# One core, two transformer blocks: the spatial stage written out by halves of the tokens, with some low parts subtracted by GpSimd

## The reference

```
proj = x @ w_in_2 + b_in_2            # u, v (part A, 512 each), a, b (part B, 512 each)
u, v = gelu(u), gelu(v)
v = layer_norm(v per head of 128, ln_a_g, ln_a_b)
v = tril(w_spatial[head]) @ v (per chunk of 128 tokens) + b_spatial[head]
part_a = u * v                         # "gated rows"
y = a * sigmoid(b)
y = causal_depthwise_conv(y, 31 taps, conv_b_w) + conv_b_b
part_b = silu(layer_norm(y over 512 channels, ln_b_g, ln_b_b))   # "conv rows"
out = concat(part_a, part_b) @ w_out_2 + b_out_2
x = layer_norm(alpha * x + out, ln1_g, ln1_b)
```

## Time and profile before

| | us |
|---|---|
| Median of 3 runs | 4498.53 |
| Lowest, highest | 4498.35, 4501.0 |
| Profiled execution | 4507.0 |
| Its span | 4505.3 |
| Busy PE, PEld, DVE | 3978.4, 3237.4, 2283.2 |
| Busy POOL, ACT | 1930.4, 1161.4 |

### The profile page before, as it was taken

How to read it: one execution, slowest core, us unless ns; L and a number is a source line. 1 busy time by engine, 2 the same in 40 slices (tenths; PEclk the granted TensorE clock), 3 DMA queues, 4 the chain that set the end, 5 groups by cost and what they waited for, 6 DMA issues and landing times.

```text
span 4505.3 us, 51892 instructions
## 1 busy us (share of the span) xinstructions
PE 3978.4 (88%) x18898; PEld 3237.4 (72%) x18898; DVE 2283.2 (51%) x3082; ACT 1161.4 (26%) x1863; POOL 1930.4 (43%) x754
## 2 busy tenths in 40 slices
PE   4778979999999899999997999999977467999997
PEld 3557767787887777777775778787866246888886
DVE  4763364344344655544545421222688876545556
ACT  3222122111114444443432211111321123222221
POOL 2323338455652412222212755564456244544551
PEclk9888979999999999999976999999988778999998
DMA  4320002223220110110100111111010010111111
GB/s 176 104 67 29 29 28 63 87 84 102 86 68 22 41 33 24 33 34 29 33 19 29 44 50 42 51 51 42 26 40 28 9 46 20 56 42 42 56 47 47
DMA packets 235628, 220.82 MB, mean 49 GB/s; under 512 B 11189, under 2 KB 188499, under 8 KB 234468
## 3 DMA queue, kind: packets, MB, share of 16 engines
q1 hardware_dynamic: 212401, 167.21, 12.3%
q10 hardware_dynamic: 23090, 51.74, 3.4%
HBM read 214.66 MB, written 4.26 MB: 49 GB/s over the span
## 4 chain that ended last, share of the span: by engine, by line
PE 74%; DVE 16%; issue 4%; ACT 3%; DMA 1%; POOL 0%; ACTq 0%; SPq 0%; DVEq 0%; POOLq 0%
PE PS L613 9%; PE PS L615 9%; PE PS L614 9%; PE PS L753 5%; PE PS L755 5%; PE PS L754 5%; PE PS L640 4%; DVE CX L2429 4%; PE PS L641 4%; PE PS L642 4%; PE PS L1066 3%; DVE QSQ L2241 2%; DVE ADMS L1862 1%; PE PS L1036 1%; PE PS L998 1%
## 5 line engine op out<-in xcount | busy, mean ns | idle before, releaser
L2671 POOL TENSOR_SCALAR WH<-RAW 128x1024 fp32r<-128x1024 f32 (+1 forms) x247 | 730.1, 2956 | 1427.2 <-PE PS L642 614.8
L613 PE MATMUL PS<-UH,WH 128*128 128x512 f32 (+1 forms) x2192 | 877.7, 400 | 25.4 <-POOL WL L2673 12.1
L615 PE MATMUL PS<-UH,WL 128*128 128x512 f32 (+1 forms) x2192 | 868.5, 396 | 0.0
L614 PE MATMUL PS<-UL,WH 128*128 128x512 f32 (+1 forms) x2192 | 862.7, 394 | 0.0
L1873 DVE TENSOR_TENSOR X<-PS,X 128x512 f32<-128x512 f32 x656 | 444.2, 688 | 493.7 <-PE PS L755 411.0
L2673 POOL TENSOR_TENSOR WL<-RAW,WH 128x1024 fp32r<-128x1024 f32 (+1 forms) x247 | 615.8, 2493 | 20.6
L613 PEld LDWEIGHTS PS<-UH,WH 128*128 128x128 f32 (+1 forms) x2192 | 417.5, 190 | 117.4 <-issue 15.7
L615 PEld LDWEIGHTS PS<-UH,WL 128*128 128x128 f32 (+1 forms) x2192 | 415.7, 190 | 98.4
L614 PEld LDWEIGHTS PS<-UL,WH 128*128 128x128 f32 (+1 forms) x2192 | 416.9, 190 | 93.4
L753 PE MATMUL PS<-WH,HH 128*128 128x512 f32 x1024 | 405.7, 396 | 33.6 <-DVE HL L2158 18.0
L755 PE MATMUL PS<-WL,HH 128*128 128x512 f32 x1024 | 400.3, 391 | 0.0
(11 more groups left out here) (343 smaller groups left out, 7307.3 us busy)
## 6 DMA issues: line engine op xcount, KB each, us to landing
RAW<-in_mlp_w_dram SPq DMA_DIRECT2D x128, 512.0 KB, 3.9
ADM<-in_ada_w_dram ACTq DMA_DIRECT2D x96, 256.0 KB, 3.1
RAW<-in_w_up_dram SPq DMA_DIRECT2D x44, 512.0 KB, 3.9
ADR<-in_ada_w_dram ACTq DMA_DIRECT2D x12, 1024.0 KB, 5.1
RAW<-in_w_down_dram SPq DMA_DIRECT2D x22, 512.0 KB, 3.3
RAW<-in_ev_w_in_dram SPq DMA_DIRECT2D x20, 512.0 KB, 4.0
ADS<-in_ada_w_dram SPq DMA_DIRECT2D x8, 1024.0 KB, 16.1
WR<-in_od_w_in_dram SPq DMA_DIRECT2D x16, 512.0 KB, 4.5
```

Source lines behind the costliest of these rows:

```text
L613: pe.matmul(bank(b)[0:width], wh, xh, start=(k == 0), stop=False)
L614: pe.matmul(bank(b)[0:width], wh, xl, start=False, stop=False)
L615: mm = pe.matmul(bank(b)[0:width], wl, xh, start=False, stop=(k == NK - 1))
L2671: pool.tensor_scalar(WH[slot][:, 0:n], r[:, 0:n], 1.0, None, ALU.mult).then_inc(S("w_hi"), 1)
```

## The change

The two loops of four rounds are gone. The stage is one list of items written out for all engines (SP_ITEMS), for one half of the tokens (512) after the other as far as the data allow:

- PE makes b and a of two channel groups for both halves, then of the other two, then u of the first half, v, the mixing, u of the second half (its weights are loaded again), and the output rows as items of 12 products that sum over all four channel groups: conv rows of the first half, gated rows of both halves, conv rows of the second half. The weights for conv rows are loaded twice.
- The conv runs on DVE alone, 31 taps for each group and half, 512 columns each, two groups in turn; a tap waits for the tap before the last. Products, mixings, statistics and additions are put between taps at given places. POOL's three taps are gone.
- The conv's norm takes its statistics with tokens on partitions: PE transposes CX (t_conv), DVE takes statistics, ACT normalises to YT, PE transposes back (t_back), ACT takes silu twice (rounded and exact).
- The head's factors of v are no longer applied to v. ACT normalises v, and factor and offset go into the bias and the mixing's eviction (mix_bias, mixed).
- Low parts: POOL subtracts those of the gated rows of both halves (mix_low) and of the first half's conv rows (silu_low); DVE those of the second half's conv rows.
- The residual factor of X: in this stage POOL does all eight blocks, blocks 0 to 3 ahead of the fifth tile, 4 to 7 ahead of the ninth; in the last stage DVE does two and POOL six.
- ACT issues eight small loads more at the program's start.

```diff
--- before.py
+++ after.py
...
+RES_DVE = {1: 4, 2: 4, 3: 4, 4: 0, 5: 2}
...
+SP_ITEMS = ([(m, c, h) for c0 in (0, 2) for h in range(2) for c in (c0, c0 + 1) for m in "ba"] +
+            [("u", c, 0) for c in range(4)] + [("v", p, t) for p in range(2) for t in range(4)] +
+            [("v", 0, t) for t in range(4, 8)] + [("v", 1, 4)] + [("m", c, 0) for c in range(4)] +
+            [("v", 1, t) for t in range(5, 8)] + [("u", c, 1) for c in range(4)] + [("m", c, 1) for c in range(4)] +
+            [(s, h, mh, t) for s, h in (("y", 0), ("x", 0), ("x", 1), ("y", 1)) for mh in range(2) for t in range(4)])
...
+            for c in range(4):
+                tile(tile_m(w_in, lambda it, c=c: c * P + 1536), ("b", c, 1))
+                tile(tile_m(w_in, lambda it, c=c: c * P + 1024), ("a", c, 1))
+            for c in range(4):
+                tile(tile_m(w_in, lambda it, c=c: c * P), ("u", c, 0))
+            for p in range(2):
+                for k0 in (0, 4):
+                    tile(tile_t(w_in, k0, [lambda it, p=p: 512 + p * 256]), ("v", p, 7))
+            for c in range(4):
+                tile(tile_m(w_in, lambda it, c=c: c * P), ("u", c, 1))
+            for mh in range(2):
+                rows(4, mh, ("y", 0, mh, 3))
+            for mh in range(2):
+                rows(0, mh, ("x", 1, mh, 3))
+            for mh in range(2):
+                rows(4, mh, ("y", 1, mh, 3))
+            plan.add("sp", 1, tiles, len(SP_ITEMS))
...
+                def t_conv(h):
+                    (d_free.wait_at(ND), a_free.wait_at(NA))[h]
+                    pe.wait_ge(S("sp_tap"), 4 * CONV_B * (h + 1))
+                    for t in range(4):
+                        b = t_bank(("c", h, t))
+                        for c in range(4):
+                            mm = pe.transpose(b[:, c * P:(c + 1) * P], CX[:, c, t * P:(t + 1) * P], IDENT[:, :])
+                        mm.then_inc(S("t_done"), 1)
...
+                def row_item(x, h, t, w, mh):
+                    o = bank(d_bank())
+                    k = slice((4 * h + t) * P, (4 * h + t + 1) * P)
+                    for c in range(4):
+                        wh, wl = (i[:, (c % 2) * HALF:(c % 2 + 1) * HALF] for i in w[c // 2])
+                        pe.matmul(o, x[:, c, k], wh, start=(c == 0), stop=False)
+                        pe.matmul(o, x[:, 4 + c, k], wh, start=False, stop=False)
+                        mm = pe.matmul(o, x[:, c, k], wl, start=False, stop=(c == 3))
+                    mm.then_inc(done, 1)
...
+                pe.wait_ge(S("wst_ready"), 1)
+                b = t_bank(("s", 0))
+                pe.matmul(b, ONES[:, :], WST[:, :, :].rearrange("p a b -> p (a b)"), start=True, stop=True)\
+                    .then_inc(S("t_done"), 1)
+                for c in range(4):
+                    u_item(tile(), 0)
                 pe.wait_ge(S("brow_in"), 16)
+                v = []
+                for p in range(2):
+                    v.append((tile(), tile()))
+                    for t in range(4):
+                        token_item(*v[p], t, extra=BROW[0:1, 256 * p:256 * p + 256])
+                        if (p, t) == (1, 1):
+                            t_conv(0)
+                for p in range(2):
+                    for t in range(4, 8):
+                        token_item(*v[p], t, extra=BROW[0:1, 256 * p:256 * p + 256])
+                        if (p, t) == (1, 4):
+                            pe.wait_ge(S("t_free"), T_AT["c", 0, 3] + 1)
+                            mix(0)
+                for c in range(4):
+                    u_item(tile(), 1)
+                    if c < 2:
+                        t_back(0, 2 * c, 2 * c + 1)
+                mix(1)
+                pe.wait_ge(S("ys_ready"), 4)
+                for mh in range(2):
+                    w = tile(), tile()
+                    for t in range(4):
+                        row_item(UL, 0, t, w, mh)
+                pe.wait_ge(S("sm_ready"), 4)
                 w = []
                 for h in range(2):
+                    if h:
+                        pe.wait_ge(S("sm_ready"), 8)
+                    for mh in range(2):
                         if h == 0:
+                            w.append((tile(), tile()))
                         for t in range(4):
+                            row_item(UH, h, t, w[mh], mh)
+                t_conv(1)
+                t_back(1, 0, 1, 2, 3)
+                pe.wait_ge(S("ys_ready"), 8)
+                for mh in range(2):
+                    w = tile(), tile()
+                    for t in range(4):
+                        row_item(UL, 1, t, w, mh)
+                        i = 4 * mh + t
+                        if 3 <= i < 7:
+                            t_u(5, 0, 2 * i - 6, 2 * i - 5)
 
             def ffn(fresh):
                 ph = PH["ffn"]
...
+                def conv_norm(h):
+                    act.wait_ge(S("lb_var"), h + 1)
+                    act.activation(LBR[:, :], MVB[:, :, 1], ACT.Sqrt, bias=EPSL[:, :]).then_inc(S("lb_std"), 1)
+                    act.wait_ge(S("lb_r"), h + 1)
+                    for t in range(4):
+                        act.activation(YT[:, t, :], t_take(("c", h, t)), ACT.Identity, bias=LBN[:, t:t + 1],
+                                       scale=LBR[:, t:t + 1]).then_inc(S("t_free"), 1)
...
+                v_gelu(0, 0, 1, 2, 3)
+                v_gelu(1, 0, 1, 2, 3)
+                v_gelu(0, 4)
+                conv_norm(0)
+                v_gelu(0, 5)
+                v_norm(0)
+                v_gelu(0, 6, 7)
+                v_gelu(1, 4, 5, 6)
+                round_mix(0)
+                v_gelu(1, 7)
+                u_gelu(0, 1)
+                silus(0, 0, 1)
+                v_norm(1)
+                u_gelu(1, 1)
+                silus(0, 2, 3)
+                u_gelu(2, 1)
+                u_gelu(3, 1)
+                round_mix(1)
+                conv_norm(1)
+                silus(1, 0, 1, 2, 3)
...
+                def conv(c0, h, between):
+                    mine.wait_at(0)
+                    for i in range(2 * CONV_B):
+                        for f, *args in between.get(i, []):
+                            f(*args)
+                        if i >= 2:
+                            dve.wait_ge(S("sp_tap"), taps[0] - 1)
+                        c, k = c0 + i % 2, CONV_PAD - i // 2
+                        x = YB[c][:, k + h * HALF:k + (h + 1) * HALF]
+                        w, y = pv("conv_b_w_2", 4 * k + c), CX[:, c, :]
+                        if i < 2:
+                            ins = dve.tensor_scalar(y, x, w, pv("conv_b_b_2", c), ALU.mult, ALU.add)
+                        else:
+                            ins = dve.scalar_tensor_tensor(out=y, in0=x, scalar=w, in1=y, op0=ALU.mult, op1=ALU.add)
+                        ins.then_inc(S("sp_tap"), 1)
+                        taps[0] += 1
...
+                product(0, 0)
+                ul(4, 1, 0, 1, 2, 3)
+                product(1, 0)
+                ul(4, 1, 4, 5, 6, 7)
+                conv(0, 0, {12: [(product, 0, 1)], 26: [(product, 1, 1)], 40: [(product, 2, 0)], 54: [(product, 3, 0)]})
+                conv(2, 0, {2: [(mask,)], 6: [(product, 2, 1)], 20: [(product, 3, 1)], 32: [(mix_bias,)]})
+                v_stats(0, 0)
+                conv_stats(0)
+                v_stats(0, 1)
+                conv(0, 1, {2: [(conv_inverse, 0)], 8: [(v_inverse, 0)], 18: [(mixed, 0, 0, 1, 2, 3)], 
+                            30: [(v_stats, 1, 0), (v_stats, 1, 1)], 36: [(v_inverse, 1)], })
+                x_ready(4, 0)
+                x_ready(4, 1)
+                adds = [("y", 0, i) for i in range(8)] + [("x", 0, i) for i in range(8)] + [("x", 1, i) for i in range(8)]
+                steps = {8 + 2 * i: [(add, *a)] for i, a in enumerate(adds)}
+                conv(2, 1, {0: [(mixed, 1, 0, 1, 2, 3)], **steps})
+                conv_stats(1)
                 stats(0, 1, 2, 3)
+                conv_inverse(1)
+                silu_low(1, 0, 1, 2, 3)
+                xhat(0)
+                for i in range(8):
+                    add("y", 1, i)
+                    if 4 <= i:
+                        ul(5, 0, 2 * i - 8, 2 * i - 7)
+                gd.skip(len(SP_ITEMS))
...
+            def mix_low(h):
+                for c in range(4):
+                    pool.wait_ge(S("smh"), 4 * h + c + 1)
+                    pool.tensor_tensor(UH[:, 4 + c, half(h)], UU[:, c, :], UH[:, c, half(h)].bitcast(F32),
+                                       ALU.subtract).then_inc(S("sm_ready"), 1)
+
+            def silu_low(h):
+                for c in range(4):
+                    pool.wait_ge(S("t_free"), T_AT["d", h, c] + 1)
+                    pool.tensor_tensor(UL[:, 4 + c, half(h)], VS[:, c, :], UL[:, c, half(h)].bitcast(F32),
+                                       ALU.subtract).then_inc(S("ys_ready"), 1)
 
...
+                        if j in (4, 8) and ph["name"] == "sp":
+                            resid(4, j - 4, 4)
```

(4 more changed lines are left out.)

554 lines of the change are left out of this document (238 added, 316 removed).

## The result

The changed kernel takes 4434.14 us (median of 4 runs, 4425.99 to 4438.01) beside 4499.05 for the kernel before in the same series: a ratio of 0.9853, 95% interval 0.9836 to 0.987. It is faster by 65 us, where 111 were forecast, and lies 2 us above the upper end of the forecast range (4350 to 4432). The profiled execution is 4437.64 us, its span 4435.9. The forecast for a profiled execution was 4396, so 41.6 us are missing, and the trace says where.

The account below looks back on a forecast made before the run. The prediction took the stage for a DVE chain with badly overlapped PE work. Its parts summed to 411 us against 512, 101 less, plus 10 in the last stage: 4498.5 - 111 = 4387 us; 8-in-10 range 4350 to 4432.

Parts of the forecast that it names:

- PE's work hardly changes: Rewritten stage: products follow each other after 0.227 us, PE's sum about 305 us, so PE alone doesn't set it.
- rival of dear taps: Rewritten stage: taps at 0.79 us each (27 us more) and 3.1 us a tile (15): 4429; chance 0.17.
- Head: Stage's start, from the MLP's end: first conv taps wait for eight DVE operations beside GpSimd's blocks of X; 42 us.
- First half's taps: First half's conv: 124 taps 84 us, products, mask and bias 6, tiles 29, GpSimd on X 17; 135 us.
- bound of 0.79: Upper end for a 512-column tap: half a 1024-wide tap, 0.71, plus 0.08 us for each instruction's fixed cost.
- rival of one tap per GpSimd operation: Beside taps: each GpSimd operation lets one tap through; middle parts 420 us instead of 292, total 4515; chance 0.03.
- Transposes: Between the halves: transposes, two token items, gelu and statistics until the first second-half tap; 16 us.
- Second half to the end of the second mixing: Second half's first pair: 62 taps 42 us, mixings 11, statistics 4, waits 12, tiles about 12; 81 us.
- Last pair with the additions: Second half's last pair: taps 42 us, 24 additions 15, six tiles 15, GpSimd's low parts 4; 76 us.
- Tail: Stage's end: conv transposes, statistics, normalising, silus, eight output items, until the last stage's first item; 61 us.
- The last stage's start: Last stage: with two blocks of X on DVE instead of four, between 0 and 14 us less, taken as 10.
- The start loads: Program's start: ACT's eight more small loads are hidden, at most a few us if they hold up the parameter load.

Follow-up runs that it names:

- padded kernel: Changed kernel with 32 bytes of padding behind the table of column vectors, so everything behind it starts at a multiple of 64 again: 4404.05 us, ratio 0.9769.
- aligned_wait_last: Padded changed kernel (4404 us) in which each tap waits for the tap just before it instead of the one before that: 4416.2 us, ratio 0.9801.
- before_shift64: Kernel before with the weight slots and all behind the vector table 64 bytes later, distance from UH 73472: 4501.39 us, ratio 0.9978.
- after_aligned: The padded kernel: changed kernel with 32 bytes of padding behind the table of column vectors; 4404.05 us, ratio 0.9769.

## Why the prediction was wrong, and where it was right

The step that failed is "PE's work hardly changes ... one product follows another after 0.227 us", and with it the silent assumption that everything outside the edits keeps its time. The pace of a product depends on where its operands lie, the change moved one of them, and 0.229 became 0.2333 over 6768 products outside the stage. Rows 10 show products with both operands in slots and scratch; I took their pace for all, while those that stream UH and UL ran at 0.229 even before. The diff has the line that makes the vector table one step wider, and I read it as bookkeeping.

With the pad the ratio is 0.9769 instead of 0.9853; the forecast was 4387 / 4498.5 = 0.9752, one in the last digit below the padded kernel's interval (0.9753 to 0.9785). That closeness is in part luck. The pad doesn't bring back the placement of before, it gives a better one, worth 0.2% to the kernel before. At equal placement the change is worth 94 to 97 us by the times, where 111 were forecast. The measured 4434 also lies near the 4429 of the rival of dear taps, but not by its mechanism: free taps take 0.66, not 0.79.

Step by step, from the padded kernel's trace, in which nothing but the placement differs (counts and lengths of single operations are from the changed kernel's, where said):
- Head: forecast 42, measured 37.9. First half's taps: 135 and 136.3. Taps at 0.68 against 0.66; twelve tiles, forecast 29, hold taps up for 30.7; eight operations on X, forecast 17, for 16.5: right, each price and not only the sum. The bound of 0.79 had no row behind its 0.08 for what each instruction costs; a tap that waits for the one directly in front takes 0.76 (aligned_wait_last). The rival of dear taps is out. The rival of one tap per GpSimd operation was right about the operations with two inputs, where no more than the one held tap gets through, and wrong about the first operation of each tile, which lets three taps through; that keeps the whole far from its 420 us.
- Transposes: 16 and 13.7. PE's longest waits are for the mask and for the transposes, 21.8 and 13.8 us, forecast 15 and 9.
- Second half to the end of the second mixing: forecast 81, measured 92.0. Its tiles were taken at 12 us. In the changed kernel the 60 taps of this stretch take 59.95 us, 20 more than free ones. 26 GpSimd operations stand beside them, eight tiles and ten low parts; the low parts, 4.6 of the 20 us, were in the sum only for the last pair. The two mixings take 15.2 us (16 operations, some held up too) where 11 were taken, and DVE's waits are 9 of the 12 forecast. This term was mis-sized by 11.
- Last pair with the additions: 76 and 83.0. In the changed kernel 60 taps take 63.0 us (forecast 42, with 19 for what tiles and low parts hold up), the additions 16.4 (forecast 15), the pair's first two operations 2.9, and DVE waits 4.9 us for PE's output, which was not in the sum. (These lengths overlap by 0.08 us where two operations follow directly.) PE's wait for free banks came, but at 7.6 us it was short. Mis-sized by 7.
- Tail: 61 and 58.2.
- The last stage's start: forecast 10, of which undoing shows 3.4 in the traces and nothing in the times. The wait fell as said, but I looked at one wait and not at what stands late next.
- The start loads cost nothing that stands out of the spread ahead of the stage, as forecast.

Stage and last stage together: 111 were forecast, and at equal placement (before_shift64 against after_aligned) the traces show 92.9 + 5.9 = 98.8. The difference, 12 us, is the error of the reasoning about the two stages; the other 30 us that were missing in the first trace are the placement.

## What to carry to other kernels

When a change grows, shrinks or reorders an allocation, compare the pace of products in a stretch that it doesn't touch before anything else. Here 32 bytes were worth 31 us between two traces of the changed kernel and 36 between two kernels of one series, and the cure was a pad that made the distance between the operands 73472, a multiple of 256. Where a DVE chain of two-input operations sets the time, work given to GpSimd is paid with what it holds DVE up. In this stage that was 1.8 us for an operation of 1024 columns with two inputs, and DVE did the same operation in 1.2. A long wait of PE beside such a chain was no reserve here: moving its cause forward changed nothing.

## What the runs showed of the hardware that was not expected

- Back-to-back products with 512 moving columns at the full clock take 0.2267, 0.229 or 0.2333 us, by the distance in SBUF from the moving rows to the weight blocks (0, 192, or 224, 64 and 128 modulo 256). The Trainium skill (SBUF — State Buffer, section "SBUF: two separate sides") says that TensorE's accesses never wait on another engine. That may hold, but a product's own two operands are not independent of each other in these runs: 882 against 865 products in 200 us.
- In the kernel before, the slow placement cost 26 us in the last stage (814.7 against 787.9), in the changed kernel 12 us (788.8 against 776.7), for the same products. The pace alone is 9 us of the 26 (2112 products at 0.0044, an estimate). In the old kernel PE waits 19 times for DVE's additions there, 34.2 us in all, where it waited once for 20.2: 14 us more. Why was not tried.

```profile
PE PS L640 <- DVE X L1873: 34.2, 19, 20.0
```

- A tap that waits for the one directly in front takes 0.76 us instead of 0.66. The Trainium skill (VectorE: DVE Perf Modes, section "The DRAIN you can't avoid"), which the prediction weighed, says of eight copies that a semaphore after each costs nothing extra; here the stage got 19.3 us longer. The same section adds that an operation which nothing holds starts earlier than the rule says, which the prediction left out and the 0.66 us of the free taps bear out (one such tap is 0.74 long).
- DVE and GpSimd hold each other up by their inputs and not by being busy. A tap with two rows from SBUF waits out a two-input operation of GpSimd (2.9 us instead of 0.74), an operation that takes one of its rows from PSUM doesn't (0.74), and a one-input operation of GpSimd holds one tap for 0.8 us.
